# Differential attention: output projections of heads 0 to 5 in pairs of heads, each pair spread over two later heads

## The reference: what is computed

```python
# D = 1024, 8 heads, head dim 64, two maps per head; latents 512, context 256
q, k, v = split(h @ wqkv)                  # q, k: (n, 8, 2, 64); v: (n, 8, 128)
q_l, k_l = apply_rope(q_l), apply_rope(k_l)
p = softmax(q k^T / 8)                     # one per map; latent queries see context and latents
p = p[:, :, 0] - lam * p[:, :, 1]
o = einsum('bhqk,bkhe->bqhe', p, v)        # (n, 8, 128)
o = rmsnorm(o, subln) * (1 - lam_init)     # over the 128 of a head
y = o.reshape(n, 1024) @ wo
h = h + gate * y                           # latents and context, each with a gate of its own
```

## Time and profile before

| | |
|---|---|
| three runs, us | 2621.54, 2616.43, 2616.13 |
| median, us | 2616.43 |
| span of the profiled execution, us | 2620.7 |
| time of the profiled execution around its span | not given; the nearest run is 2621.54 |
| granted TensorE clock, mean over the span | 0.972 |
| busy: TensorE, VectorE, ScalarE, GpSimd | 93%, 60%, 40%, 13% |
| instructions | 35948 |

### The profile page before, as it was taken

How to read it: one execution, slowest core, us unless ns; L and a number is a source line. 1 busy time by engine, 2 the same in 40 slices (tenths; PEclk the granted TensorE clock), 3 DMA queues, 4 the chain that set the end, 5 groups by cost and what they waited for, 6 DMA issues and landing times.

```text
span 2620.7 us, 35948 instructions
## 1 busy us (share of the span) xinstructions
PE 2449.5 (93%) x14115; PEld 2107.4 (80%) x14115; DVE 1563.9 (60%) x3020; ACT 1056.3 (40%) x1878; POOL 345.6 (13%) x241
## 2 busy tenths in 40 slices
PE   7999989999998999998899999999889897999998
PEld 6788877788787878776788888889778786888887
DVE  4566657878867777777756544445545456533334
ACT  5455534223254555555521211113555545422223
POOL 2222210000031221221000000002222322000001
PEclk9999999999999999999899999999999999899999
DMA  4222125555521111111234333331212122232331
GB/s 121 61 65 58 47 83 160 174 157 176 175 75 43 41 35 39 41 33 41 73 104 130 104 110 108 119 115 46 53 44 57 45 53 57 76 109 85 100 109 49
DMA packets 240617, 220.73 MB, mean 84 GB/s; under 512 B 26620, under 2 KB 207650, under 8 KB 240450
## 3 DMA queue, kind: packets, MB, share of 16 engines
q1 hardware_dynamic: 240450, 218.45, 27.4%
HBM read 216.17 MB, written 2.24 MB: 83 GB/s over the span
## 4 chain that ended last, share of the span: by engine, by line
PE 73%; DVE 13%; ACT 7%; issue 5%; DMA 1%; SPq 0%; POOL 0%; DVEq 0%; POOLq 0%; ACTq 0%
PE ps L369 23%; PE ps L370 22%; PE ps L371 22%; ACT whi L400 1%; PE ps L2492 1%; DVE FR L539 1%; PE ps L2944 1%; ACT FA L2585 1%; DVE FA L673 1%; DVE hT L2665 1%; ACT FR L534 1%; DVE wlo L411 1%; DVE FA L2705 1%; PE ps L1114 1%; ACT FA L3013 1%
## 5 line engine op out<-in xcount | busy, mean ns | idle before, releaser
L369 PE MATMUL ps<-Uh,whi 128*128 128x512 f32 (+2 forms) x2544 | 898.3, 353 | 17.5 <-ACT FA L2604 5.9
L370 PE MATMUL ps<-Ul,whi 128*128 128x512 f32 (+2 forms) x2544 | 884.5, 348 | 0.0
L371 PE MATMUL ps<-Uh,wlo 128*128 128x512 f32 (+2 forms) x2544 | 883.7, 347 | 0.0
L369 PEld LDWEIGHTS ps<-Uh,whi 128*128 128x128 f32 x2544 | 487.5, 192 | 84.7 <-issue 18.0
L371 PEld LDWEIGHTS ps<-Uh,wlo 128*128 128x128 f32 x2544 | 486.3, 191 | 59.5
L370 PEld LDWEIGHTS ps<-Ul,whi 128*128 128x128 f32 x2544 | 487.2, 192 | 57.0
L400 ACT ACTIVATE whi<-raw 128x1024 fp32r<-128x1024 f32 (+3 forms) x211 | 297.8, 1411 | 539.8 <-PE ps L371 539.6
L411 DVE TENSOR_TENSOR wlo<-raw,whi 128x2048 fp32r<-128x2048 f32 (+2 forms) x117 | 239.3, 2046 | 258.5 <-ACT whi L400 258.1
L369 PE MATMUL ps<-FR,whi 128*128 128x512 f32 (+1 forms) x864 | 302.4, 350 | 14.3 <-DVE FR L539 7.8
L411 POOL TENSOR_TENSOR wlo<-raw,whi 128x1024 fp32r<-128x1024 f32 (+1 forms) x94 | 227.3, 2418 | 666.3 <-ACT whi L400 665.5
L370 PE MATMUL ps<-FR,whi 128*128 128x512 f32 (+1 forms) x864 | 298.6, 346 | 0.0
(11 more groups left out here) (347 smaller groups left out, 2999.2 us busy)
## 6 DMA issues: line engine op xcount, KB each, us to landing
FA<-in_ada_w_dram SPq DMA_DIRECT2D x192, 256.0 KB, 2.8
raw<-in_ffn_w_gate_up_dram SPq DMA_DIRECT2D x44, 1024.0 KB, 5.1
raw<-in_ffn_w_down_dram SPq DMA_DIRECT2D x24, 768.0 KB, 4.6
raw<-in_w_in_dram SPq DMA_DIRECT2D x29, 512.0 KB, 3.9
raw<-in_da_wqkv_dram SPq DMA_DIRECT2D x24, 512.0 KB, 3.7
raw<-in_na_wqkv_dram SPq DMA_DIRECT2D x24, 512.0 KB, 3.8
raw<-in_w_ffn_gate_dram SPq DMA_DIRECT2D x11, 1024.0 KB, 5.4
raw<-in_w_ffn_up_dram SPq DMA_DIRECT2D x11, 1024.0 KB, 5.4
```

The lines of the kernel that those rows point to most:

```text
L369: e.matmul(out, ah, bh, start=start, stop=False)
L370: e.matmul(out, ah, bl, start=False, stop=False)
L371: return e.matmul(out, al, bh, start=False, stop=stop)
```

## The change

It does these things.

- Heads 0 to 5 go in pairs (0, 1), (2, 3), (4, 5). A chunk holds 256 rows of `wo` (the rows of both heads) by 512 columns, and a pair has two chunks. A step `pair` makes one block of 128 columns for 512 and 256 rows; each result sums both heads in its PSUM bank with six matmuls. Steps 0 to 3 of the pair (j - 2, j - 1) stand in even head j, steps 4 to 7 in head j + 1. So head 1 has no output steps, heads 2 to 6 have four steps, and head 7 has the last four steps of the pair (4, 5) and the four `out` steps of head 6.
- `doh` and `dol` exist twice (`dof`): the second copy lies in the free columns of the other hi and lo buffers.
- The planned pauses of head 7, costs (`sums` 1.3 to 2.1, `first` 5.8 to 5.6) and latenesses are other numbers, so the engines' orders are others.

```diff
-        self.doh, self.dol = self.hi[0][:, 1024:1792], self.lo[0][:, 1024:1792]
+        self.dof = [tuple(x[1 - i][:, 1024:1792] for x in (self.hi, self.lo)) for i in range(2)]
...
-              "ones": (("end_root", 0.1),) + tuple((("hi", c), 2.2 + 0.95 * c) for c in range(KC))}
-END_VECTOR = {"out3": (("columns", -3.0),) + tuple((("add", n), 0.45 * n - 2.4) for n in range(KC)) +
+              "ones": (("end_root", 0.1),) + tuple((("hi", c), 3.0 + 0.95 * c) for c in range(KC))}
+END_VECTOR = {"out3": (("columns", -3.4),) + tuple((("add", n), 0.45 * n - 2.4) for n in range(KC)) +
...
-            out = [(2, ("out", j - 1, n2)) for n2 in range(4)]
-            split = [(0, ("split", j - 1, "out"))]
-            tail = [(1.3, ("sums", j - 1, 0))]
-            if j < 7:
-                fill = qk[0:6] + tail + qk[6:] + v[0:2] + out[0:1] + v[2:3] + split + out[1:3] + v[3:] + out[3:]
-            else:
-                fill = [(5, ("pause", 7, 0))] + tail + split + [(3, ("pause", 7, 1))] + out + [(4, ("pause", 7, 2 + n)) for n in range(4)]
-        else:
-            fill = qk + v
+        split, tail = [(0, ("split", j, "out"))], [(2.1, ("sums", j - 1, 0))]
+        pair = [(2.1, ("pair", j - 1 - j % 2, 4 * (j % 2) + n)) for n in range(4)]
+        if j == 0:
+            fill = qk + v
+        elif j == 1:
+            fill = qk[0:3] + tail + qk[3:] + v
+        elif j == 7:
+            out = [(2, ("out", 6, n2)) for n2 in range(4)]
+            fill = split + pair + tail + [(2.0, ("pause", 7, 0))] + split + [(3.0, ("pause", 7, 1))] + out + [(2.5, ("pause", 7, 2 + n)) for n in range(4)]
+        elif j % 2:
+            fill = split + pair + qk[0:2] + tail + qk[2:] + v
+        else:
+            fill = qk[0:6] + tail + qk[6:] + v[0:2] + pair[0:1] + v[2:3] + split + pair[1:3] + v[3:] + pair[3:]
...
+        elif what == "pair":
+
+            if x % 4 == 0:
+                co = K.use(w, wsrc(wo, (j - 1) * P, (j + 1) * P, x * P, x * P + 512), 2, 512)
+                w.wait_ge(*K.at("d_fin_lo", j))
+            c0 = x % 4 * P
+            for i, (t0, t1) in enumerate((SL, SC)):
+                b = K.xbank["d", "out", j, x, i] = spare(1.0)
+                o = K.hold(w, b, ("d_add", j, x, i))[:, 0:t1 - t0]
+                for k in range(2):
+                    oh, ol = K.dof[k]
+                    t = mm3(e, o, co[1][:, k, c0:c0 + P], co[2][:, k, c0:c0 + P], oh[:, t0:t1], ol[:, t0:t1], k == 0, k == 1)
+                t.then_inc(*K.ev("d_out", j, x, i))
+            K.used[co[0]] = ("d_out", j, x, 1)
...
-               "sums": (("ln", 0.1), ("root", 0.2), ("fin_hi", 3.9)),
-               "scores": (("exp", 1.4), ("share", 4.0)), "turn": (("t_hi", 0.1),), "values": (("o_out", 0.1),)}
+               "sums": (("ln", -0.7), ("root", 0.2), ("fin_hi", 3.9)),
+               "scores": (("exp", 2.2), ("share", 4.0)), "turn": (("t_hi", 0.1),), "values": (("o_out", 0.9),)}
...
-            w.wait_ge(*K.was("d_out", j - 1, 7, 1))
-            halve_scalar(K, e, K.oraw, K.doh, ("d_fin_hi", j))
+            w.wait_ge(*K.was("d_out", j - 1 - j % 2, 7, 1))
+            halve_scalar(K, e, K.oraw, K.dof[j % 2][0], ("d_fin_hi", j))
...
-               "turn_v": (("tv_lo", 0.8),), "sums": (("scale", 2.9), ("fin_lo", 4.8)), "out": (("out", 0.1),),
-               "scores": (("max", 0.1), ("inv", 3.2), ("norm", 5.0)), "turn": (("t_lo", 0.8),)}
+               "turn_v": (("tv_lo", 0.8),), "sums": (("scale", 1.4), ("fin_lo", 4.8)), "out": (("out", 0.1),), "pair": (("pair", -0.7),),
+               "scores": (("max", 0.9), ("inv", 3.2), ("norm", 5.0)), "turn": (("t_lo", 0.8),)}
```

More of the change, by code:

```diff
@@ L2207 @@
 END_SCALAR = {"out3": tuple((("sq", n), 0.45 * n - 1.8) for n in range(KC)),
-              "ones": (("end_root", 0.1),) + tuple((("hi", c), 2.2 + 0.95 * c) for c in range(KC))}
-END_VECTOR = {"out3": (("columns", -3.0),) + tuple((("add", n), 0.45 * n - 2.4) for n in range(KC)) +
+              "ones": (("end_root", 0.1),) + tuple((("hi", c), 3.0 + 0.95 * c) for c in range(KC))}
+END_VECTOR = {"out3": (("columns", -3.4),) + tuple((("add", n), 0.45 * n - 2.4) for n in range(KC)) +
               tuple((("sum", n), 0.45 * n - 1.2) for n in range(3, KC, 2)),
-              "ones": tuple((("scaled", c), 1.7 + 0.95 * c) for c in range(KC)) + tuple((("lo", c), 2.7 + 0.95 * c) for c in range(KC))}
-END_GPSIMD = {"out3": tuple((("sum", n), 0.45 * n - 1.2) for n in range(2, KC, 2))}
+              "ones": tuple((("scaled", c), 1.7 + 0.95 * c) for c in range(KC)) + tuple((("lo", c), 3.1 + 0.95 * c) for c in range(KC))}
+END_GPSIMD = {"out3": tuple((("sum", n), 0.45 * n - 1.4) for n in range(2, KC, 2))}
 def end_out_tensor(K, e, w, s, i, spare, wh, wl, oh, ol):
@@ L2351 @@
             ("turn", 7, 5): (("ones", 7, 0),)}
-DIFF_COST = {**END_COST, "sums3": 0.5, "lat": 5.4, "ctx": 2.8, "rot": 0.5, "turn_v": 0.7, "sums": 1.3, "out": 2.1, "first": 5.8, "second": 2.9}
+DIFF_COST = {**END_COST, "sums3": 0.5, "lat": 5.4, "ctx": 2.8, "rot": 0.5, "turn_v": 0.7, "sums": 1.3, "out": 2.1, "pair": 2.1, "first": 5.6, "second": 2.9}
 def diff_cost(what, j, x):
@@ L2367, in diff_chain @@
     if what == "sums3":
-        return ("values", j, 2 * x + 1), 1.6
-    first, late = {"out3": ("sums3", 4.0), "ones": ("out3", 3.0), "turn": ("scores", 6.6), "values": ("turn", 4.0), "rot": ("lat" if j else "second", 2.5), "out": ("sums", 8.0)}.get(what, (None, 0.0))
-    return (first, j, x), late
+        return ("values", j, 2 * x + 1), 3.1
+    first, late = {"out3": ("sums3", 4.0), "ones": ("out3", 3.0), "turn": ("scores", 6.6), "values": ("turn", 4.0), "rot": ("lat" if j else "second", 2.5), "out": ("sums", 8.0), "pair": ("sums", 8.0)}.get(what, (None, 0.0))
+    return (first, j, 0 if what in ("out", "pair") else x), late
 def diff_keys(u):
@@ L2457, in diff_tensor @@
             w.wait_ge(*K.at("d_fin_lo", j, x))
-            end_out_tensor(K, e, w, "d", x, spare, co[1], co[2], K.doh, K.dol)
+            end_out_tensor(K, e, w, "d", x, spare, co[1], co[2], *K.dof[1])
             K.used[co[0]] = ("e_out", "d", KC - 1, x)
@@ L2657, in diff_vector @@
             w.wait_ge(*K.at("d_fin_hi", j))
-            halve_vector(K, e, K.oraw, K.doh, K.dol, ("d_fin_lo", j))
-        elif what == "out":
-            for n in (2 * x, 2 * x + 1):
+            halve_vector(K, e, K.oraw, *K.dof[j % 2], ("d_fin_lo", j))
+        elif what in ("out", "pair"):
+            for n in (2 * x, 2 * x + 1) if what == "out" else (x,):
                 for i, (t0, t1) in enumerate((SL, SC)):
@@ L2663, in diff_vector @@
                     w.wait_ge(*K.at("d_out", j, n, i))
-                    w.wait_ge(*(K.was("d_add", j - 1, n, i) if j or i else K.at("b1_scaled", n, 1)))
+                    w.wait_ge(*(K.was("d_add", j - 1 - j % 2, n, i) if j > 1 or i else K.at("b1_scaled", n, 1)))
                     e.scalar_tensor_tensor(out=hv, in0=bank("out", j, n, i)[:, 0:t1 - t0], scalar=K.mod[0][:, 16 + n, i:i + 1], in1=hv,
@@ L2675, in diff_vector @@
             w.wait_ge(*K.at("d_fin_hi", j, x))
-            halve_vector(K, e, K.oraw[:, p.t0:p.t1], K.doh[:, p.t0:p.t1], K.dol[:, p.t0:p.t1], ("d_fin_lo", j, x))
+            halve_vector(K, e, K.oraw[:, p.t0:p.t1], *(t[:, p.t0:p.t1] for t in K.dof[1]), ("d_fin_lo", j, x))
         elif what == "columns" or isinstance(what, tuple):
```

16 lines of the change are left out of this document (8 added, 8 removed).

## The result

The changed kernel takes 2584.6 us (median of 4 runs, 2580.09 to 2590.64) against 2616.28 (2615.74 to 2621.54). The ratio of the runs is 0.9872, 95% interval 0.9854 to 0.9890: 1.3% faster, where 0.6% was forecast.

What follows compares the result with a forecast made beforehand. The prediction took TensorE to bound the kernel, with time to win only where it waits or runs at half clock. Its terms, -10.2 - 7.2 - 1.6 + 3.0 = -16.0 us, took 2616.4 to 2600.4, range 2592 to 2611.

Steps and rivals of the forecast that it cites:

- Part 4: New engine orders, waits and weight loads: late times only reorder, charged 3 us; bounds nothing and 24 pair steps at 0.98 us.
- Part 1: Heads 2 to 6: halved adds and banks remove TensorE's named waits, 1.4 us a head, 7.2 us; bounds 0 and 12.9.
- Part 2: Head 1 loses its output steps: four steps, 8.8 us, and 1.4 us of waits, 10.2 us shorter.
- Part 3: Head 7, second scores to its own output projection: four more steps fill idle time; 33.0 us, 1.6 less.
- the 5.4 us behind L2604: TensorE's waits in the loop for the copy of the attention output: unchanged, set by the chain from sums to fin_lo.
- More: Rival: the rest of the loop's idle goes too (12.9, not 7.2) and orders cost nothing; 2591.7 to 2594, chance 0.08.
- VectorE as the bound of head 7: Rival: in head 7 VectorE keeps its 7.7 us of waits, the stretch takes 38.3 us; 2605.7, chance 0.15.
- Slower: Rival: VectorE stands at each of 24 pair adds, 0.98 us a step, 23.5 us; 2628.1, chance 0.06.
- Weights, the second copy of the halves, the fetches: Pair's weight loads in 2 KB runs are covered by earlier fetching; the second copy brings no cost, no gain: nothing.
- the row: Heads 1 to 6: profiled granted clock 1.00 despite short waits, so relieving banks gains nothing by the clock.
- given back: Rival: the last projection's new piece order puts half its work at half clock, costing 8.7 us; 2609.1, chance 0.09.
- the waits staying: Rival: banks are not what TensorE waited for, only the shift from head 1 to 7 pays; 2609.0, chance 0.12.

Runs made afterwards that it cites:

- e1: Changed kernel with the latenesses and planned costs of the kernel before, except those that only place the fill; pairs and placement stay: 2600.44 us, ratio 0.9938.
- e5: Kernel before, with each output-projection add to hT over half of its columns, so part of the output is missing: ratio 0.9981.
- e11: Changed kernel, but each head of a pair has its own PSUM bank and its own add, over half of its columns: ratio 0.9904.
- e3: Changed kernel, but each head of a pair has its own PSUM bank and its own full add; placement and orders stay: ratio 0.9962.
- e10: Changed kernel with a second, idle add (the bank times zero) ahead of each add of a pair step: ratio 0.9967.
- e6: Changed kernel with only the latenesses of max (0.1) and exp (1.4) set as in the kernel before: ratio 0.9928.
- e7: Changed kernel with the latenesses of ln, scale and the copy of the attention output as in the kernel before: ratio 0.9882.
- e4: Changed kernel, but the last four pair steps stand at the end of head 6 and head 7 has its old fill: ratio 0.9931.
- e9: Changed kernel, with each add to hT in pair and out steps over half of its columns: ratio 0.9877.
- e12: Changed kernel with max and exp planned 0.6 later still (1.5 and 2.8): ratio 0.9969.

## Why the prediction was wrong

**Part 4, orders: the step that failed.** It said that the late times "only reorder" and added 3 us for all of them, with "nothing" as the best case. Measured with the pairs in place they are worth 13.0 us the other way (e1). Without that term the sum was -19.0, and e1, which is the change without the new orders, is 18.6 us shorter in the stage. That its median of 2600.44 equals the forecast of 2600.4 is partly chance: the forecast had +3 for orders in it, and e1's heads 1 to 6 give 21.9 where parts 1 and 2 said 17.4, head 7 +2.6 where part 3 said -1.6, two misses that cancel. The rows for this were at hand and not read: the prediction put the stage at 850 to 1300 us, where it is 812 to 1249, so head 0 lay outside its windows, and the first turn of head 0 waited 4.57 us for a norm that stood in VectorE's queue behind two maxima and then ran into GpSimd's split. The earlier trace rows even showed such a wait in head 7 (4.43 us), and the prediction never asked what stood ahead of that norm. The price went to the pair's add being planned early, and VectorE never stood long at it (0.5 us in all at the adds of pair and out in the changed kernel).

**Part 1, 7.2 us in heads 2 to 6:** the mechanism was half right. Banks are what separate steps lose (e5, e11), and the halved VectorE time pays where steps stand together (e3, e10). Under old orders heads 2 to 6 are shorter by 13.8 us; they hold two steps less, 4.4 us of matmuls, so 9.4 us are waits, inside the bounds of 0 to 12.9. The named waits undercount: a wait that the trace puts at 0.25 to 0.53 us seems to come with small gaps around it that name no releaser (argued, not shown). A step's length up to the next work (2.80 against 2.2) would have said 0.6 x 20 = 12.

**Part 1, the 5.4 us behind L2604 "stays": wrong.** It is 2.6 now and 7.5 with max and exp early (e6), 4.0 with the old tail (e7): planned numbers set it, not the chain that I named.

**Part 2, head 1:** right, and rather more than forecast. Two of its four steps lie before the next scores and two behind, and head 1 is 7.9 us shorter, of which 4.4 are two steps; the other 3.5 are waits, forecast at 1.4.

**Part 3, head 7, 33.0 us for the stretch:** 35.56 was measured (34.63 before). The move hides four steps at no cost (e4: 10.1 us, where the sum had 8.8 + 1.6). The gap stands elsewhere now: 3.09 us at 1181.01, for the split of the transposed attention weights. So two of the signs that the prediction named did not come: a gap over 1 us stands before the out steps of head 6, and the clock of the stretch is 0.95 and not 1.00.

```profile
1181.01 0.36 PE L369 MATMUL ps<-FR 128*128 128x256 f32 x1 [3.09 <-DVE FR L539]
```

**The rivals.** "More" (2591.7 to 2594) had the right side and too small a size. VectorE as the bound of head 7 is there with 1.3 us at most (e9). "Slower", an order of VectorE that makes TensorE wait, exists with other instructions: e12, with max and exp later, is 23.8 us longer, and over its stage TensorE waits 22.4 us for VectorE's splits and adds, against 7.2 in the changed kernel. I gave orders a sign without a row that showed one.

**Weights, the second copy of the halves, the fetches:** as said, no wait names them in the stage.

**The clock.** For these two kernels the row held, and what the Trainium skill says of cycling PSUM banks (TensorE: Matmul & The Clock Gate, "A second HAM failure mode: psum-queue depth-cycling") did not: the granted clock was 1.00 with 15.5 us of short waits in 300, and is 1.00 with 4.0 in 252 now, so relieving the banks gave nothing back there by the clock. e5 shows that it can happen: in its head 2 the clock fell once behind waits of 0.26 and 1.09 us, and the head was 1.0 us longer. What the clock gave back lies in heads 0 and 7, behind the long waits.

**Readings and sums that were off.** The window from 900 to 1200 us holds the last quarter of head 1's period and heads 2 to 6, 5.3 heads and not six: its named waits are 1.6 us a head, not 1.4, which makes 8.1 in place of 7.2, and the bound of 12.9 is 14.5. The 4.3 us "above the median" compare a span with a time; the nearest run, 2621.54, lies 5.1 above. "More" ends at 2594.7 with the 3 us paid, and "given back" with the waits staying at 2617.7. None of these moves the forecast by more than about a microsecond.

Nothing that was run and computes all of the output beats the changed kernel. New orders are worth 5.5 us more with the pairs (13.0) than without (7.5), and this lies in head 7: they shorten it by 4.2 with the pairs (57.3 to 53.1) and lengthen it by 2.0 without (54.7 to 56.7). Why they do was not tried and stays open, as does why max and exp at 1.5 and 2.8 cost as much as 23.8 us; collisions with GpSimd are not it, since e12's norms run into it no more than the changed kernel's.

## What to carry to other kernels

Where engines work through hand-planned queues, read each engine's order as a part of the kernel of its own: for every wait of the bound engine, ask what stands in the releaser's queue ahead of the releaser, and whether the releaser itself is longer than its like. Two planned numbers were worth 8 us here without any other change. Summing partial products in PSUM paid above all where such steps stand close together, through the time of the engine that empties the banks (25.8 us more with doubled adds, collisions and clock included, 7.9 with doubled banks and short adds); where they stand apart it is a microsecond a head. Work without dependences belongs into the stage that cannot fill itself.

## What was not expected of the hardware

VectorE's norm, which reads both of its large operands from SBUF, waited for GpSimd: begun inside a GpSimd instruction it ended 0.81 to 0.83 us behind that instruction, 28 times out of 28, and took up to 3.16 us in place of 1.02. The maxima (0.95 us) and the adds to hT (0.75 and 0.48 us), which read PSUM, kept their durations beside GpSimd. So the place of an instruction in VectorE's order also decides what it meets on GpSimd.

A wait costs more than its length. With 4.57 us of idle time in it the stretch had a granted clock of 0.87, and the six transposes behind the wait took 1.54 us, against 0.88 behind a wait of 1.38. Code that is the same in both kernels, ahead of the stage, differed by 9.0 us between the two profiled executions, of which 7.9 are busy time of the same 4160 matmuls, with a mean clock of 0.97 against 0.99 and of 0.94 against 1.00 in one stretch of it:

```profile
60.00:122.00 62.00, 57.36 (x394) 51.04 (x393) 33.82 (x87) 29.55 (x71) 16.40 (x6) 0.94 0.29 78
```
```profile
60.00:122.00 62.00, 56.06 (x409) 49.99 (x408) 36.95 (x92) 30.73 (x73) 16.43 (x6) 1.00 0.27 77
```
